# Sample attention over cached keys: values requested ahead of the same sequence's keys

## The reference, cut to what matters

```python
# window attention of the samples: 3 dilations, kcat = 1024 cached keys + 8 new ones
def dilated_step(q, kcat, vcat, window, dil, w_buf):
    idx = w_buf + jnp.arange(t_new)[:, None] - dil * jnp.arange(nk)[None, :]
    kg = jnp.take(kcat, idx, axis=1); vg = jnp.take(vcat, idx, axis=1)
    s_ = jnp.einsum('bthd,btjhd->bthj', q, kg)
    ...                                   # mask, softmax over j
    o = jnp.einsum('bthj,btjhd->bthd', p, vg) / den
# memory attention of the samples: 4 heads of 128 over 256 keys
def mem_attend(hn, mem_k, mem_v, w_xq, g_xq, w_xo):
    s = jnp.einsum('blhd,bmhd->bhlm', q, mem_k) * (X_HEAD_DIM ** -0.5)
    p = jax.nn.softmax(s, axis=-1)
    o = jnp.einsum('bhlm,bmhd->blhd', p, mem_v)
```

## Time and profile before

| what | us |
|---|---|
| median of 3 runs | 3493.07 (3488.86 to 3499.3) |
| the profiled execution | 3486.0, span of the trace 3484.0 |
| `sw`: first request of SP to the outputs' | 1651.16 to 1765.67 |
| `sm`: first request of SP to the outputs' | 2184.82 to 2223.09 |
| PE busy over the span | 3027.7 |
| DMA, mean rate over the span | 158 GB/s |

### The profile page before, as it was taken

The page is one execution under the profiler, slowest core; times in us unless marked ns, Lnnn a source line. Parts: engine busy times, 40 slices in busy tenths (PEclk is TensorE's granted clock), DMA queues, the critical chain, the costliest instruction groups (busy, mean ns, idle before and its releaser), DMA issues. The chain is left out here.

```text
span 3484.0 us, 63255 instructions
## 1 busy us (share of the span) xinstructions
PE 3027.7 (87%) x22834; PEld 2629.0 (75%) x22879; DVE 1778.9 (51%) x2685; ACT 1471.7 (42%) x2924; POOL 448.3 (13%) x430
## 2 busy tenths in 40 slices
PE   7999999979998699945667999599519999999998
PEld 7999999978887588844436887388418888888886
DVE  5154055545554355543325775244337767776572
ACT  5112145335555455531212331256216655565452
POOL 1000000000000000000410000111152222222222
PEclk9999999989999899976778999799759999999999
DMA  5333333233344211121943342533239889989792
GB/s 167 117 116 132 143 129 117 72 96 118 124 139 146 67 44 62 54 84 32 304 138 124 125 137 76 183 135 134 81 106 354 298 299 324 315 286 321 231 321 55
DMA packets 300611, 549.18 MB, mean 158 GB/s; under 512 B 81669, under 2 KB 137619, under 8 KB 299886
## 3 DMA queue, kind: packets, MB, share of 16 engines
q1 hardware_dynamic: 261326, 406.64, 34.4%
q0 software_dynamic: 34864, 137.67, 12.6%
q10 hardware_dynamic: 4224, 2.10, 0.2%
HBM read 436.53 MB, written 143.43 MB: 166 GB/s over the span
## 5 line engine op out<-in xcount | busy, mean ns | idle before, releaser
L136 PE MATMUL pj_pu<-pj_w,pj_nT 128*128 128x256 f32 (+3 forms) x1088 | 307.2, 282 | 0.0
L137 PE MATMUL pj_pu<-pj_w,pj_nT 128*128 128x256 f32 (+3 forms) x1088 | 306.4, 282 | 0.0
L138 PE MATMUL pj_pu<-pj_w,pj_nT 128*128 128x256 f32 (+3 forms) x1088 | 305.7, 281 | 0.0
L3139 ACT ACTIVATE ex_gate<-ex_gate_raw 128x2048 fp32r<-128x2048 f32 x64 | 120.5, 1913 | 208.0 <-DMA ex_gate_raw<-in_w_gate 111.6
L137 PEld LDWEIGHTS pj_pu<-pj_w,pj_nT 128*128 128x128 f32 (+1 forms) x1088 | 202.5, 186 | 0.0
L138 PEld LDWEIGHTS pj_pu<-pj_w,pj_nT 128*128 128x128 f32 (+1 forms) x1088 | 202.5, 186 | 0.0
L136 PEld LDWEIGHTS pj_pu<-pj_w,pj_nT 128*128 128x128 f32 (+1 forms) x1088 | 202.1, 186 | 0.1
L716 ACT ACTIVATE att_prob<-att_score,att_res 128x256 f32<-128x256 f32 (+1 forms) x384 | 127.6, 443 | 142.6 <-DVE att_res L752 142.6
L3202 DVE TENSOR_TENSOR ex_down<-ex_down_raw,ex_down 128x2048 fp32r<-128x2048 f32 x64 | 146.6, 2291 | 79.3 <-ACT ex_down L3139 62.1
L3202 DVE TENSOR_TENSOR ex_gate<-ex_gate_raw,ex_gate 128x2048 fp32r<-128x2048 f32 x64 | 144.0, 2287 | 83.2 <-ACT ex_gate L3139 83.2
L136 PE MATMUL pj_pu<-pj_nT,pj_w 128*128 128x384 f32 (+2 forms) x480 | 175.3, 365 | 0.0
(11 more groups left out here) (566 smaller groups left out, 7895.1 us busy)
## 6 DMA issues: line engine op xcount, KB each, us to landing
ex_gate_raw<-in_w_gate SPq DMA_DIRECT2D x64, 1024.0 KB
ex_up_raw<-in_w_up SPq DMA_DIRECT2D x64, 1024.0 KB, 10.0
ex_down_raw<-in_w_down SPq DMA_DIRECT2D x64, 1024.0 KB, 10.9
out_win_k<-in_cache_k POOLq DMA_DIRECT2D x8, 2032.0 KB, 12.9
out_win_v<-in_cache_v POOLq DMA_DIRECT2D x8, 2032.0 KB, 13.6
tmp_att<-att_res POOLq DMA_DIRECT2D x48, 264.0 KB, 4.5
pout_att<-tmp_att SPq DMA_DIRECT2D x16, 792.0 KB, 4.5
pj_raw<-in_w_in SPq DMA_DIRECT2D x24, 512.0 KB
```

Source lines behind the costliest of these rows:

```text
L136: pe.matmul(out, ah, bh, start=start, stop=False)
L137: pe.matmul(out, ah, bl, start=False, stop=False)
L138: return pe.matmul(out, al, bh, start=False, stop=stop)
L3139: act.activation(half[p][:, 0, part(p, h)], raw[p][:, part(p, h)], ACT.Copy).then_inc(E[p + "_hi"], 1)
```

## The change

On SP, `attend_sample` asks for the values of a sequence ahead of that sequence's keys, in both stages. The waits inside `keys` and `values` stay as they are. No other engine's list differs.

```diff
                 if not mem:
                     sp.dma_start(mult[:], t["sw_mult"]).then_inc(E["mult_in"], 16)
-                for b in range(B):
-                    if b + 1 < B:
-                        keys(b + 1)
+                values(0)
+                for b in range(1, B):
                     values(b)
+                    keys(b)
                 sp.wait_ge(E["none_ok"], 1)
```

## The result

The changed kernel takes 3591.83 us (median of 4 runs, 3588.43 to 3598.85), the kernel before 3494.52 us (4 runs): a ratio of 1.0282, 95% interval 1.0259 to 1.0305. It is slower by 97 us.

What follows compares the result with a forecast made beforehand. Transfers were taken to bound sw (DMA share 0.99), while in sm they come early enough. sw +56 and sm +42 give +98 us: 3584 on the profiled execution's 3486.0, 3591 measured like the median; range 3560 to 3626.

Steps and rivals of the forecast that it cites:

- The mechanism: Both stages: SP's keys request stands behind a wait for the product of b-2, so PE idles while values and keys travel.
- P in `sw`: Time from one product to the next in sw: 20.5 us, with 18.0 and 22.6 as ends.
- T + 12.7: In sw, all keys have landed 12.7 us after T, the end of a product; near ones up to 2.8 us sooner.
- The clock's term: In sw, TensorE's lower clock adds up to 4.6 us a sequence; about half was taken, 18.0 becoming 20.5 us.
- the +68 us: Both stages' sum by the Trainium skill page's figures, some 30 us smaller; set aside because the trace decides.
- Start and end of `sw`: Product of 0 ends at 1689.5 instead of 1680.75; at the stage's end 2 us more of softmax show.
- `sm`: Product to product 9.6 us (8.8 to 10.7), start +5.5 us; stage +42 us, ends +37 and +49.
- A: Rival: faster, as early values end sw's 17.2 us of waits for values; 3476 us; chance 3%.
- B: Rival: unchanged at 3493 us, because sw's queue stays full and the order of equal loads cannot matter; chance 4%.
- C: Rival: only sw pays, as two key buffers keep keys ahead in sm; +56 us, 3549 us; chance 6%.
- D: Rival: worse, PE at the lower clock through both stages and POOL's loads colliding; +124 us and more, 3620; chance 9%.

Runs made afterwards that it cites:

- sw_only: New order of requests in sw alone, the order of before kept in sm, against the kernel before: 3544.13 us, ratio 1.0148.
- sm_only: New order of requests in sm alone, the order of before kept in sw, against the kernel before: 3539.52 us, ratio 1.0130.
- three_values: Changed kernel with three value buffers instead of two, so values of b wait for the product of b-3: 3512.26 us, ratio 1.0049 to the kernel before.
- keys_then_values: Changed kernel with the loop's two calls swapped, keys of b then values of b: 3505.10 us, ratio 1.0032 to the kernel before.
- hold_keys_first: Changed kernel, but SP after waiting for the product of b-2 asks for keys first, then values: 3553.14 us, ratio 1.0173 to the kernel before.
- warm: Changed kernel plus 84 unread identity transposes on PE in sw while it waits for keys of 1 to 7: 3590.54 us, ratio 1.0284 to the kernel before.
- two_keys_before: Kernel before, with its old order of requests, given two key buffers in sw: 3493.41 us, ratio 1.0006.
- two_keys_after: Changed kernel given two key buffers in sw too: 3586.88 us, ratio 1.0276 to the kernel before.
- the kernel with 11 matmuls: Changed kernel with PE kept busy during sw's key waits by 11 matmuls of 512 columns instead of 84 transposes: 3593.65 us, ratio 1.0286 to the kernel before.

## Why the prediction was right

*The mechanism.* SP's request for the values of b stands right behind a product, its wait is put down to the product, the keys' request behind it, as the prediction said; the sign and the place follow from that. `sw_only` and `sm_only` show the two stages' prices separately, `three_values` that it is the wait for the product that costs. How the price divides follows from three runs that differ by one step each: 12 us for the values' earlier place (`keys_then_values`; in `sm` a wait for an earlier product is in it), 50 us for the hold (`hold_keys_first`), and 35 us for the values' bytes ahead of the keys under that hold.

*P in `sw`*, forecast 20.5 us: five of six are 20.3 to 20.8, one is 23.8, the mean 126.24 / 6 = 21.0. The sum came out, its terms did not; that they cancel is luck. The prediction had all keys at T + 12.7, then 5.3 us to the end of the product at the full clock, and 2.5 us for the lower one. The trace has the turning start at T + 10.8, with the near keys, and all 28 transposes run from there without a break; then 9.5 us to the end of the product, of which the warmed sequence, 7.4 us (1707.71 to 1715.15), makes 2.1 us the clock's. The far keys landed 8.4 to 8.6 us after their requests at 1700.5 and 1701.0, some 12 us after the product and close to the 12.7, but they never bound: the near transposes were still running then, and in `warm` no turning of 3.44 us broke off for them either. So the step from landing to far transposes was wrong as the prediction put it: the near keys bind, 1.9 us ahead of T + 12.7, and the near transposes, which it left out of the path, make the rest 9.5 us instead of 5.3 + 2.5 = 7.8. The clock's term was right in size (2.1 for 2.5). Its place is the turning, which runs mostly at the lower clock; the probabilities, scores and product run at the full one.

The Trainium skill's figures ("DMA: Bandwidth & Descriptors", section Specifications: 0.6 us to the first byte, about 358 GB/s) would land values and near keys, 2.66 MB, after an estimated 8.0 us. The trace has 10.8 and does not agree; the +68 us that the prediction put beside its own sum by that page falls with it.

*Start and end of `sw`*: +9.6 us where +8.8 was taken. The end was wrong: -1.1 instead of +2. The softmax of 7 shows no longer than before, 1.55 us for 1.41, and the last product runs at the full clock, 1.87 us, where before it took 3.13. First the row before, then the two after:

```profile
1762.08 3.13 PE L2165 MATMUL sw_pv<-sw_vv,sw_pT 128*32 128x128 f32 x56 [0.90 <-DVE sw_pT L2097]
...
1825.01 0.98 PE L2152 MATMUL sw_pp<-sw_ident,sw_pr 128*128 128x128 f32 x7 [1.55 <-ACT sw_pr L2035]
1826.90 1.87 PE L2165 MATMUL sw_pv<-sw_vv,sw_pT 128*32 128x128 f32 x56 [0.90 <-DVE sw_pT L2097]
```

Together `sw` has +56.7 us for +56.

*`sm`*: P 9.85 for 9.6. The keys came a little sooner (5.04 us for 5.4), and the rest took longer (4.8 us for 4.2), at the lower clock throughout, where the prediction had taken the value of a turning partly slow. The start is +6.8 for +5.5. Together +44.8 for +42. The sum of both is +101.5 in the traces where +98 was forecast; in the medians the difference is 97. That the forecast of 3591 meets the 3591.83 so closely is in part luck.

*The rivals.* A (faster, the values are early): the 17.2 us of waits for values did vanish, and waits for keys took their place. `three_values` and `keys_then_values` show that even without the long hold the earlier values gain nothing. B (only bytes count) falls for the new order, whose DMA share is 0.56; for the old one it holds, as `two_keys_before` shows. C (only `sw` pays) falls by `sm_only`. D (worse) came by half and not as a time: in `sm` TensorE did stay at the lower clock (clock share 0.51), but in `sw` no later load of POOL's fell on the keys. The third was asked for at 1707.81 and had landed by 1717.42, in the time in which PE was at work:

```profile
1707.81 0.92 POOL L2186 DMA_DIRECT2D ow_raw<-in_w_xq  x1 [0.30 <-POOL ow_w L131]
1717.42 0.56 POOL L2190 DMA_DIRECT2D ow_gx<-in_g_xattn  x1 [8.69 <-DMA ow_raw<-in_w_xq]
```

In `hold_keys_first` that same load did fall on the keys. And in the one sequence with late keys, 23.83 us, POOL did nothing:

```profile
1778.81:1802.64 23.83, 9.71 (x108) 7.94 (x107) 4.85 (x11) 3.68 (x7) 0.00 (x0) 0.64 0.46 134
```

## What to carry to other kernels

On a queue that issues in order, a wait in front of one load holds every load behind it. Before a request is moved ahead of another, look up what its wait waits for and where that stands in the consumer's list: here it was the last step before the work that needs the next load. Put the load that the consumer needs first in front (swapping two lines won back 85 of 97 us), and where the DMA share of a stage is already near 1.0, expect nothing from an earlier request.

## What the runs showed of the hardware

Late keys go together with a packet of a queue that the profile calls instruction (q8) among the loads. In the changed kernel, an ordinary wait for keys (1738.0 to 1748.6); the queue's kind, its packets, MB, share of 16 engines:

```profile
q1 hardware_dynamic: 1572, 3.02, 91.8%
```

And the late one (1778.9 to 1792.9), first the DMA share in tenths and GB/s in 40 equal slices of 0.35 us:

```profile
DMA  1009144999999999999999999999999995200000
GB/s 47 0 18 176 53 70 158 357 386 369 392 427 386 369 380 258 217 246 269 187 234 369 386 369 357 357 345 340 316 252 258 199 263 129 35 6 23 29 23 23
...
q1 hardware_dynamic: 1653, 3.16, 77.2%
q8 instruction: 1, 0.02, 0.4%
```

Most engines are done 2 us before PE goes on; in the last six slices 6 to 35 GB/s move, about what one of 16 engines has of 386 (24 GB/s). So it looks as if PE waits for one engine that lags behind the others. Over the changed kernel and the two warmed ones, the ten waits between two products that had such a packet ended 11.4 to 14.2 us after the product; of the eight without, seven ended after 10.5 to 11.0 us and one after 11.4. The traces of `sw_only` and `two_keys_after` agree: the one wait with such a packet ended after 14.1 us, the eleven without after 10.4 to 11.6. In the kernel with 11 matmuls all six had one, and the rows of its late wait shown above (1719.0 to 1732.2) are:

```profile
q1 hardware_dynamic: 1657, 3.17, 82.7%
...
q8 instruction: 1, 0.02, 0.6%
```

This would say where the gain of the faster turnings went, but no run took the packets away or doubled them: that they are the cause is not shown. Few instructions did not help, as that kernel shows.

A load of POOL's costs PE time where it falls on the keys, as in `hold_keys_first` (12.0 us of waiting for 5.8), and nothing here where it falls into the time in which PE works: with POOL's load in the sequence and without, the period is the same. The first two sequences of `sw`, in the columns of the earlier trace rows:

```profile
1697.22:1717.56 20.34, 9.45 (x107) 7.70 (x107) 4.84 (x11) 3.67 (x7) 11.27 (x4) 0.66 0.83 260
1717.56:1737.92 20.36, 9.58 (x108) 7.80 (x107) 4.85 (x11) 3.68 (x7) 17.96 (x4) 0.66 0.53 158
```
